# One landing slot for weights fewer, two half slots for rounded parts more, and pieces split one step further ahead

## The reference

```
for layer in (0, 1):                       # block 1
    h = rms_norm(x, mix_pre_g[layer])
    m = diff_attention(h, a_w_qkv, a_w_o)  if layer == 0 else
        stick_breaking_attention(h, b_w_q, b_w_o, rms_norm(x, kv_norm_g) @ kv_w)
    x = x + rms_norm(m, mix_post_g[layer])
    gate, up = split(rms_norm(x, ffn_pre_g[layer]) @ ffn_w_gate_up[layer])
    x = x + rms_norm((silu(gate) * up) @ ffn_w_down[layer], ffn_post_g[layer])
# block 2: h = x + positions, hc = context (256 rows of its own)
mods = silu(c) @ w_ada + b_ada ; mods_c = silu(c_ctx) @ w_ada + b_ada
h, hc = ffn_sublayer(h, ..., w_ffn1_in, w_ffn1_out), ffn_sublayer(hc, ..., the same weights)
p = modulate(rmsnorm(h), ...) @ w_in       # q, k, v, gates, o, u, vs, ga, gb; q to gates for hc too
h_m = mLSTM in chunks of 128 rows, both directions, context first
y_a = sigmoid(o) * head_layernorm(h_m) ; y_b = spatial_gating(gelu(u), gelu(vs))
h = h + gate * (sigmoid(ga) * (y_a @ w_branch_a) + sigmoid(gb) * (y_b @ w_branch_b)) @ w_out
h = ffn_sublayer(h, ..., w_ffn2_in, w_ffn2_out)
return rmsnorm(h, g_final)
```

## Time and profile before

| | |
|---|---|
| median of 3 runs | 1581.02 us (1580.82 to 1582.62) |
| the profiled execution's own time | 1582.28 us |
| its span | 1580.5 us |
| busy: TensorE, its weight loads, VectorE, ScalarE, GpSimd | 98%, 89%, 66%, 52%, 9% |
| mean granted clock of TensorE | 0.998 |
| read from memory | 306.7 MB |
| landing of a load after its issue, median: most kinds; `w_ada`, `w_in` | 5.0 to 5.4 us; 7.7, 8.0 us |

### The profile page before, as it was taken

The page is one execution under the profiler, slowest core; times in us unless marked ns, Lnnn a source line. Parts: engine busy times, 40 slices in busy tenths (PEclk is TensorE's granted clock), DMA queues, the critical chain, the costliest instruction groups (busy, mean ns, idle before and its releaser), DMA issues.

```text
span 1580.5 us, 25068 instructions
## 1 busy us (share of the span) xinstructions
PE 1547.4 (98%) x10493; PEld 1402.5 (89%) x10493; DVE 1039.5 (66%) x1701; ACT 822.3 (52%) x1208; POOL 149.8 (9%) x140
## 2 busy tenths in 40 slices
PE   7999999999999999999999999999999999999997
PEld 6888999988989879998899999889888888889986
DVE  5786757866566676776675756568747876664554
ACT  4587554444479743444463565444545646364442
POOL 2220011100002110010001100101000000001000
PEclk9999999999999999999999999999999999999999
DMA  9756757766543457877655595598562565585552
GB/s 326 264 202 238 227 186 240 240 239 202 187 160 107 153 172 265 291 266 267 201 174 174 186 171 181 182 194 175 142 158 67 147 170 172 182 275 191 188 187 80
DMA packets 219808, 309.37 MB, mean 196 GB/s; under 512 B 5004, under 2 KB 146720, under 8 KB 219696
## 3 DMA queue, kind: packets, MB, share of 16 engines
q1 hardware_dynamic: 217600, 301.48, 61.4%
q0 software_dynamic: 1664, 5.84, 1.1%
q10 hardware_dynamic: 432, 0.45, 0.1%
HBM read 306.71 MB, written 1.05 MB: 195 GB/s over the span
## 4 chain that ended last, share of the span: by engine, by line
PE 82%; DVE 9%; ACT 6%; DMA 2%; issue 1%; POOL 0%; DVEq 0%; ACTq 0%
PE ps L137 79%; DVE wl L150 3%; PE ps L140 2%; ACT wh L146 1%; ACT L146 1%; ACT SA L146 1%; DMA raw<-in_w_in_dram 1%; DVE SM L160 1%; ACT SA L147 1%; DVE FT L160 0%; DVE X L160 0%; DMA raw<-in_a_w_qkv_dram 0%; DVE SA L160 0%; DMA X<-in_x_dram 0%; DVE MT L150 0%
## 5 line engine op out<-in xcount | busy, mean ns | idle before, releaser
L150 DVE TENSOR_TENSOR wl<-raw,wh 128x1024 fp32r<-128x1024 f32 x498 | 607.6, 1257 | 334.7 <-ACT wh L146 334.0
L146 ACT ACTIVATE wh<-raw 128x1024 fp32r<-128x1024 f32 x498 | 502.3, 1053 | 220.4 <-PE ps L137 122.8
L137 PE MATMUL ps<-XPf,wh 128*128 128x256 f32 x1408 | 248.4, 281 | 0.0
L137 PEld LDWEIGHTS ps<-XPf,wh 128*128 128x128 f32 x1408 | 214.7, 188 | 0.1
L137 PE MATMUL ps<-XPf,wl 128*128 128x256 f32 x704 | 197.5, 281 | 0.0
L137 PE MATMUL ps<-XPc,wh 128*128 128x256 f32 x832 | 145.5, 279 | 0.0
L137 PE MATMUL ps<-wh,HTL 128*128 128x512 f32 x352 | 137.0, 389 | 0.0
L137 PE MATMUL ps<-wl,HTH 128*128 128x512 f32 x352 | 137.0, 389 | 0.0
L137 PE MATMUL ps<-wh,HTH 128*128 128x512 f32 x352 | 136.9, 389 | 0.0
L137 PEld LDWEIGHTS ps<-XPf,wl 128*128 128x128 f32 x704 | 134.9, 192 | 0.0
L137 PEld LDWEIGHTS ps<-XPc,wh 128*128 128x128 f32 x832 | 126.0, 188 | 1.2 <-issue 1.0
(11 more groups left out here) (359 smaller groups left out, 2733.2 us busy)
## 6 DMA issues: line engine op xcount, KB each, us to landing
raw<-in_w_ffn_in_dram SPq DMA_DIRECT2D x66, 1024.0 KB, 5.1
raw<-in_ffn_w_gate_up_dram SPq DMA_DIRECT2D x44, 1024.0 KB, 5.4
raw<-in_w_in_dram SPq DMA_DIRECT2D x40, 1024.0 KB, 8.0
raw<-in_w_ffn_out_dram SPq DMA_DIRECT2D x30, 1024.0 KB, 5.0
raw<-in_ffn_w_down_dram SPq DMA_DIRECT2D x20, 1024.0 KB, 5.3
raw<-in_w_ada_dram SPq DMA_DIRECT2D x18, 1024.0 KB, 7.7
raw<-in_w_adaT_dram SPq DMA_DIRECT2D x18, 1024.0 KB, 5.0
raw<-in_a_w_qkv_dram SPq DMA_DIRECT2D x12, 1024.0 KB, 7.5
```

Source lines behind the costliest of these rows:

```text
L137: return NOTHING if self.e is None else self.e.matmul(o, l, r, start=start, stop=stop, skip_group_check=skip)
L146: return self.e.activation(o, i, fn, bias=bias, scale=scale)
L150: return NOTHING if self.e is None else self.e.tensor_tensor(o, a, b, f)
```

## The change

Two sizes and two depths.

```diff
-NRAW = 5
-NHL = 6
+NRAW = 4
+NHL = 8
...
-            def look_ahead(depth=2):
+            def look_ahead(depth=3):
...
             def norm_steps(*want):
-                look_ahead(3)
+                look_ahead(4)
```

## The result

The changed kernel takes 1711.65 us (median of 4 runs, 1709.86 to 1714.45) against 1581.82 us for the kernel before on the same chip (4 runs, 1580.82 to 1583.63): a ratio of 1.0821, with a 95% interval of 1.0801 to 1.0841. It is 130 us slower. The forecast was 1639.6, slower by 59, with a range up to 1665.

What follows compares the result with a forecast made beforehand. TensorE was taken to bound the kernel, busy 1547.4 of 1580.5 us. Terms summed to +58.6 on the profiled 1582.3, giving 1640.9; with the median 1.3 lower, the forecast was 1639.6, range 1595 to 1665.

Steps and rivals of the forecast that it cites:

- the landing slot: Plain stretches: one landing slot fewer, with splits unmoved, costs nothing, as three pieces (16 us) cover a 5.4 us landing.
- the small places and the loop: Six small places of the same patterns, +16.2 us; layer 1's gate-up loop with its close landings, +3.5 us.
- the clock: TensorE's clock drops after long idle times: three losses taken, +4.2 us, bounds 0 and 8.4.
- norm: End of layer 0's FFN: piece 80's casts stand ahead of the squares and delay the scaled rows, +5.2 us.
- OA: Layer 0's attention: piece 22's cast waits for its landing ahead of the OA that TensorE needs, +4.7 us.
- XPf: Piece 38's casts stand ahead of the eight shifted rows at 182.06 us, +4.0 us.
- GS: Woven stretch: piece 183's slow load puts its rest ahead of VectorE's rT and GS rows, +9.0 us.
- Hm: Norm before w_in: piece 207's casts stand between the square and the scaled rows, +7.2 us.
- FT: mLSTM's first step: piece 212's casts delay mqT and the FT that TensorE uses, +7.1 us.
- Loads bound it: Rival: with four slots, w_in loads limit the stretch from 1040 to 1290; 1660 to 1680 us, chance 0.13.
- Places absorbed: Rival: small places and loop give nothing, large ones two thirds, no clock term; 1603 us, chance 0.27.
- faster after all: Rival: landings come no later than their casts, so late rests go; 1577 to 1579 us, chance 0.05.

Runs made afterwards that it cites:

- after_noload: Changed kernel without loads of split pieces, ScalarE casting from a constant tile: 1590.7 us, against 1580.1 for the kernel before in the same form.
- one_place: slot_only with piece 212 (w_in) split one step earlier, ahead of mqT and two FT: 1639.0 us against 1627.6.
- slot_only: Kernel before with four landing slots and eight half slots, at the old depths 2 and 3: 1627.6 us, ratio 1.0295.
- depth_only: Kernel before with the new depths 3 and 4, at the old five landing slots and six half slots: 1664.8 us, ratio 1.0523.
- slot_quarter: slot_only with only a quarter or half of each split piece loaded, same engine instructions: 1586.4 us, against 1579.6 for the kernel before so loaded.
- early_two: Kernel before with pieces 14 and 90 split earlier (one step meant; piece 14 moved three): 1583.5 us, ratio 1.0011.

## Why the prediction was wrong

**Direction and mechanism: right.** Slower was given 0.92, by casts that wait for landings ahead of urgent work. `after_noload` shows that loads carry 120 of the 130 us, and `one_place` shows one such pair of casts at work. (The look ahead moves 393 halves forward; the prediction's 391 is off by two.) What failed are three terms of the sum: the landing slot at nothing, the small places and the loop at 17 us, and the clock at 4.

**The six named places: right in sum.** TensorE's idle time at them, after less before: norm 5.7 (forecast 5.2), `OA` 3.9 (4.7), `XPf` 5.5 (4.0), `GS` 2.6 (9.0), `Hm` 3.4 + 3.3 = 6.7 (7.2), `FT` 11.5 (7.1): 35.9 against 37.2. That the sum came so close is in part luck: the errors of `GS` and `FT`, -6.4 and +4.4, largely cancel. `GS` was over by 6; TensorE had stood just ahead of it, at a wait that I had not named (2.29 us for `LF`, first row below), and came later to it itself. The second place had another cause than the one given. Pieces 22 and 23 keep their step, so no cast was put ahead of that `OA`; its load came later, and `slot_only`, with the old order, stands there for 4.45 us too. That term belonged to the slot, which was put at nothing. `FT` was under by 4: I had put `FT` right behind the casts and left out VectorE's `MT`, which waits behind the rests. They are read from rows like these:

```profile
978.17 2.70 PE L137 MATMUL ps<-LF,C 128*128 128x4 f32 x12 [2.29 <-DVE LF L160]
```

```profile
115.13 1.65 PE L137 MATMUL ps<-kT,qT 64*128 64x256 f32 x8 [4.23 <-ACT OA L146]
```

```profile
211.68 0.77 PE L137 MATMUL ps<-XPf,wh 128*128 128x256 f32 x2 [5.45 <-issue]
```

```profile
1137.64 0.30 PE L140 MATMUL ps<-C,Hm 128*128 128x128 f32 x1 [3.43 <-DVE Hm L156]
1141.23 1.11 PE L140 MATMUL ps<-C,Hm 128*128 128x128 f32 x4 [3.28 <-ACT Hm L146]
```

**The small places and the loop: mis-sized, 17 for 53.** The terms +16.2 and +3.5 less the gain of 2.5 made 17.2. The idle time outside the six places grew by 88.9 - 35.9 = 53.0. There are not six small places. The change has 42 idle times of over half a us, against 12 before. Most are at evictions and factors I had passed over because in the trace of before nobody waited for them, for example `LF` and `kT` in the list of waits above. That each of them is a cast standing ahead for its landing I didn't trace; that they hang on the loads together is what `after_noload` shows, with 4 of the 88.9 us left. And they are spread over the kernel. Its 10493 matmuls are in the same order in all kernels, so each can be compared with itself: the one that starts at 200 us before starts 29 us late after the change, the one at 900 us 61 late, the one at 1200 us 110 late. For `slot_only` these are 25, 31 and 44, for `depth_only` 32, 46 and 75; so in the first 200 us each of the two costs by itself about what the change costs with both, which is why 46 and 84 can't be two separate losses that add.

**The clock: mis-sized tenfold, 4.2 for 41.8.** I counted one loss of 1.4 us for each of the three longest stands. The trace has far more: 19 stretches at the lower level besides the one at the end, against one before. TensorE is at work at that level for 80.9 us, before for 3.4, and half of the difference, 39 us, is nearly all of the 41.8. It is much the same in the parts: `slot_only` has 31.5 us more idle than before and 18.6 us of slower products, `depth_only` 55.5 and 27.0, the change 88.9 and 41.8 (busy times and spans of the two rows below, against 1547.4 of 1580.5). About half a us of slower products goes with each us of idle time:

```profile
span 1630.6 us, 24994 instructions
...
PE 1566.0 (96%) x10493; PEld 1413.6 (87%) x10493; DVE 1037.6 (64%) x1701; ACT 819.1 (50%) x1208; POOL 148.8 (9%) x140
```

```profile
span 1663.0 us, 25151 instructions
...
PE 1574.4 (95%) x10493; PEld 1424.7 (86%) x10493; DVE 1037.0 (62%) x1701; ACT 835.1 (50%) x1208; POOL 150.9 (9%) x140
```

My upper bound, 8.4, rested on the one dip of the trace before. There idle time was rare, so one dip said little of how many there would be, and it had followed a wait for GpSimd's `HCL`, not for a load. The rule that I set beside it, from the Trainium skill's page "TensorE: Matmul & The Clock Gate", "HAM oscillation", was the better guide, and I had read it as a bound for six places. The trace after agrees with it at its longest stand (the clock at 0.50 to 0.59 in the table above) and in that there are 19 such stretches, though not every one of the 42 idle times has one.

**"One landing slot fewer costs nothing": wrong.** It costs 46 us by itself (`slot_only`), 41 of them by landings (`slot_quarter`). I had counted the cover up to TensorE's use of the piece. What counts is the cover up to its place in ScalarE's order, two pieces before that. The Trainium skill's "DMA: Bandwidth & Descriptors", "Rules for kernel authors", wants the issue early and the wait late; the runs agree, and put 46 us on an issue one piece later with the waits unmoved.

**The gain: nothing seen.** TensorE's waits for `wl` were to vanish, and grew from 2.5 to 6.0 us. `early_two` returned nothing either, though it was no clean test.

**The rivals.** "Loads bound it" gave the nearest time (1660 to 1680), still 32 us short. It is partly right: four slots are too few for the landings by 46 us even in the old order, and the `w_in` stretch that it priced at 40 us (1040 to 1290) lost 42.5. But TensorE waited only 10 us in all for split pieces, so most of the landings reached it through the work behind the casts, which is the forecast's path. "Places absorbed" and "faster after all" are out.

## What to carry to other kernels

In an engine that works in order, moving a prefetch stage forward only helps if its inputs are surely there at the new place; otherwise it hands its wait to everything behind it. A guard should ask that a load has had time to land, not that it may start (no run here has such a guard), and the cover of a buffer is to be counted to the first engine that touches it, not to the last. And idle time of TensorE had a surcharge in this kernel, half again, so a forecast of stands has to carry it for each us and not for a few long ones.

## What was not expected of the hardware

The clock's share: an idle time of 11.4 us was followed by some 5 us at 1.2 GHz, and 31.5 us more of idle time, in stands of 4.5 us and less, came with 18.6 us of slower products. And one landing slot fewer, with no split moved ahead, cost 46 us while the median landing stayed at 5.4 and 8.1 us.
